# One core, three transformer blocks: the query and key stage of block 1 reordered, and the delta rule's row terms of block 2 made inside its projections

## The reference, cut to what matters

```python
# block 1: sparse attention beside a convolution
h = rms_norm(x, norm_mix_g)
(q, kc, vc, ks_, vs_, kw, vw, g_nsa, u_a, u_b, g_attn, g_conv) = split(h @ w_in)
q = apply_partial_rope(q)                  # 16 heads of 64; the keys kc, ks_, kw (4 heads of 64) too
k_c = silu((blocks_of_32(rope(kc)) + cmp_k_pos) @ cmp_k_w1) @ cmp_k_w2     # 31 compressed keys
v_c = silu((blocks_of_32(vc) + cmp_v_pos) @ cmp_v_w1) @ cmp_v_w2
attn = nsa_attention(q, k_c, v_c, rk(ks_), rv(vs_), rk(kw), rv(vw), gates)
conv = conformer_conv(u_a, u_b, ...)       # depthwise, 31 taps over time
# block 2: gated delta rule, 8 heads of 128
qkv = silu(causal_depthwise_conv(qkv, conv_w))       # 4 taps, 3072 channels
q = l2norm(q) * 128 ** -0.5;  k = l2norm(k)
g = -exp(a_log) * softplus(a_raw + dt_bias);  gc = cumsum(g)      # per chunk, token and head
decay = exp(gc[..., :, None] - gc[..., None, :])
m = tril(einsum(k * beta, k) * decay)                # solved per chunk, then a scan over chunks
```

## Time and profile before

| what | value |
|---|---|
| median of 3 runs | 2946.54 us (2945.48 to 2947.42) |
| the profiled execution | 2947.61 us, of which the span of the profile is 2945.8 us |
| PE busy | 2751.6 us, 93% |
| DVE busy | 1635.0 us, 56% |
| ACT busy | 1010.9 us, 34% |
| POOL busy | 1053.5 us, 36% |
| mean granted TensorE clock | 0.976 |

### The profile page before, as it was taken

One profiled execution on the slowest core, in us unless ns is written; L12 is line 12 of the kernel. 1 busy time (PEld: TensorE's weight loads), 2 busy tenths in 40 slices (PEclk: granted clock), 3 DMA queues, 4 the chain that ended last, 5 costly groups with the idle time before them and its releaser, 6 DMA issues.

```text
span 2945.8 us, 38330 instructions
## 1 busy us (share of the span) xinstructions
PE 2751.6 (93%) x13198; PEld 2259.6 (77%) x13198; DVE 1635.0 (56%) x2597; ACT 1010.9 (34%) x1750; POOL 1053.5 (36%) x463
## 2 busy tenths in 40 slices
PE   7998899999999989969998999999899999999997
PEld 5875788777888867858887777787577777778775
DVE  6967887573423376556656645435623446653353
ACT  3224555543222253433334411112425553211133
POOL 3432000144444434333423344444332224444443
PEclk9999999999999999989999999999899999999998
DMA  3242000133222222211102222222131112222222
GB/s 127 100 132 68 22 15 15 36 108 102 93 93 99 93 85 83 86 69 62 62 33 79 95 93 92 93 86 92 66 101 58 49 52 93 93 93 93 93 93 86
DMA packets 66296, 234.31 MB, mean 80 GB/s; under 512 B 7515, under 2 KB 9860, under 8 KB 66188
## 3 DMA queue, kind: packets, MB, share of 16 engines
q1 hardware_dynamic: 58176, 211.84, 20.9%
q10 hardware_dynamic: 8012, 21.05, 2.1%
HBM read 228.61 MB, written 2.16 MB: 78 GB/s over the span
## 4 chain that ended last, share of the span: by engine, by line
issue 52%; PE 33%; POOL 12%; DVE 2%; POOLq 0%; ACT 0%; DMA 0%; DVEq 0%; SPq 0%; ACTq 0%
POOL w_lo L405 11%; PE bank L2281 9%; PE bank L2283 9%; PE bank L2282 9%; PE bank L2773 2%; PE bank L2762 2%; PE bank L2460 0%; PE bank L2690 0%; POOLq L409 0%; PE bank L2443 0%; DVE big L1644 0%; PE bank L2811 0%; PE bank L2812 0%; PE bank L2797 0%; DVE big L1646 0%
## 5 line engine op out<-in xcount | busy, mean ns | idle before, releaser
L405 POOL TENSOR_TENSOR w_lo<-raw,w_hi 128x1024 fp32r<-128x1024 f32 x398 | 980.4, 2464 | 1825.9 <-ACT w_hi L496 1686.2
L2281 PE MATMUL bank<-act,w_hi 128*128 128x512 f32 x3128 | 1262.7, 404 | 94.1 <-POOL w_lo L405 26.6
L2283 PE MATMUL bank<-act,w_lo 128*128 128x512 f32 x3128 | 1232.7, 394 | 0.0
L2282 PE MATMUL bank<-act,w_hi 128*128 128x512 f32 x3128 | 1231.6, 394 | 0.0
L2281 PEld LDWEIGHTS bank<-act,w_hi 128*128 128x128 f32 x3128 | 595.6, 190 | 251.6 <-issue 91.3
L496 ACT CAST w_hi<-raw 128x1024 fp32r<-128x1024 f32 x397 | 416.4, 1049 | 939.9 <-PE bank L2283 937.6
L2283 PEld LDWEIGHTS bank<-act,w_lo 128*128 128x128 f32 x3128 | 595.3, 190 | 128.4
L2282 PEld LDWEIGHTS bank<-act,w_hi 128*128 128x128 f32 x3128 | 597.0, 191 | 118.9 <-issue 2.9
L1486 DVE TENSOR_TENSOR X<-X,bank 128x512 f32 x56 | 38.5, 688 | 250.1 <-PE bank L2283 250.0
L1823 DVE CAST act<-tmp 128x512 f32 x64 | 142.2, 2223 | 10.0 <-DVE tmp L1819 5.2
L1598 DVE SCALAR_TENSOR_TENSOR bank<-big,cols,bank 128x512 f32<-128x512 f32 x174 | 115.4, 753 | 0.0
(11 more groups left out here) (388 smaller groups left out, 2895.3 us busy)
## 6 DMA issues: line engine op xcount, KB each, us to landing
raw<-in_w_dram SPq DMA_DIRECT2D x402, 512.0 KB, 3.2
act_f<-head_rows ACTq DMA_DIRECT2D x8, 768.0 KB, 4.1
act_f<-in_cw1k_dram ACTq DMA_DIRECT2D x4, 512.0 KB, 4.2
out_dram<-X ACTq DMA_DIRECT2D x4, 512.0 KB, 2.7
cst<-in_consts_dram ACTq DMA_DIRECT2D x3, 648.5 KB, 4.2
X<-in_x_dram ACTq DMA_DIRECT2D x2, 512.0 KB, 6.3
X<-in_x_dram SPq DMA_DIRECT2D x2, 512.0 KB, 6.0
X<-big ACTq DMA_DIRECT2D x8, 128.0 KB, 2.3
```

Source lines behind the costliest of these rows:

```text
L405: pool.tensor_tensor(w_lo[:, u], raw[:, u].rearrange("p (k n) -> p k n", k=KT), w_hi[:, u].bitcast(F32), ALU.subtract).then_inc(w_lo_ready, 1)
L2281: pe.matmul(o, l_hi, r_hi, start=start, stop=False)
L2282: pe.matmul(o, l_hi, r_lo, start=False, stop=False)
L2283: return pe.matmul(o, l_lo, r_hi, start=False, stop=stop)
```

## The change

**Block 1.** The weights come in another order (`QK_ORDER`): keys and values to be compressed, then the other keys, then the queries. The swap of a chunk stands on PE behind the unit that follows the chunk's own, its rope on DVE another place later, both inside the `qk` stage; the last swap stands in `token_major`. DVE keeps the swapped chunk's product in the swap's own bank and reads the cosines from bank 7, into which ACT copies them, for the first 12 ropes. The 16 transfers of pairs are issued by ACT behind the copies 4 to 7, four each. Blocks with positions are made in four parts at places 10 to 13. Between the ropes stand 60 taps; the 48 that remain stand behind the low query parts, six each. PE's wait for the taps moves from the first compressed sum to the attention. The sums of the compression are in banks 6 and 7, and two parts of the values' sum stand ahead of the keys' sum. ACT makes the high query parts 7 to 2 inside `token_major` and 1 and 0 before the compression.

**Block 2.** `conv4` sums in banks 6 and 7; chunks 22 and 23 are done alone. `LAG` is 3; squares are summed two units earlier; the logarithms stand behind copy 19, the turning of rows on PE behind unit 21, the copies of the rows on ACT (three, from banks 2, 3, 4) behind silu 18, with the store. The loads of rows for heads 0 and 1 stand behind copy 22. The exponentials `BE`, `EGLAST`, `EGLC` stand behind the last silu. `tokens_and_scores(h)` waits for silu 17 + h.

```diff
-ROPED = [12, 13, 10, 11, 8, 9, 0, 1, 2, 3, 4, 5, 6, 7]
-SWAPS = ((2, 3, 4), (5, 6, 7), (8, 9), (10, 11), (12, 13))
+QK_ORDER = [12, 13, 14, 15, 8, 9, 10, 11, 0, 1, 2, 3, 4, 5, 6, 7]
+ROPED = [n for n in QK_ORDER if n < 14]
...
 # ACT, block 1
+                a.wait_ge(rope_table, 3)
+                a.copy(bank[7][:], COS).then_inc(rope_table, 1)
...
+                for j, chunk in enumerate(QK_ORDER):
+                    U = FIRST["qk"] + j
+                    if j:
+                        split_hi(U + 1, (U + 1) % 2)
+                    a.wait_ge(mm_done, U + 1)
+                    a.activation(QK[:, chunk], bank[U % 2][:], ACT.Copy, scale=DH ** -0.5 if chunk < 8 else 1.0).then_inc(act_read, 1)
+                    if 4 <= j < 8:
+                        a.wait_ge(roped, 2)
+                        for g in (2 * (j % 2), 2 * (j % 2) + 1):
+                            pairs_of_positions((j - 4) // 2, g)
+                    if j >= 8 and j % 2 == 0:
+                        keys_weights((j - 8) // 2)
...
                 token_major("token_major", 5, lambda k: [(V_TOK[:, k], slice(0, P))],
-                            lambda k: ACT.Sigmoid if k == 4 else ACT.Copy, lambda k: pairs_of_positions() if k == 0 else None,
-                            whole=True)
+                            lambda k: ACT.Sigmoid if k == 4 else ACT.Copy,
+                            lambda k: [query_high(n) for n in ((), (), (7, 6), (5, 4), (3, 2))[k]], whole=True)
...
+                query_high(1)
+                query_high(0)
                 a.wait_ge(cmp_sum, 1)
                 hidden_by_position(0)
...
 # ACT, block 2
-                LAG = 5
+                LAG = 3
...
+                    if k == 22:
+                        split_hi(U + 2, U % 2)
+                        a.wait_ge(rows_out, 16)
+                        load_rows(0)
+                        load_rows(1)
                     if k >= LAG:
                         silu(k - LAG)
-                    if k == 22:
+                    if k == 19:
                         tables(LOG_EXP)
                         a.wait_ge(l2_sum, 16)
...
                         tables(SILU)
+                    if k == 21:
+                        a.wait_ge(rows_tr, 1)
+                        for x in range(3):
+                            a.copy(ROWS[0:8, x], bank[2 + x][0:8, :]).then_inc(rows_kept, 1)
+                        a.wait_ge(rows_kept, 3)
+                        a.dma_start(head_rows, ROWS[0:8]).then_inc(rows_out, 16)
...
 # DVE, block 1
-                conv_taps(PER_GATE * (KT - 2), EARLY, in_psum)
...
+                def rope(k):
+
+                    chunk, swapped_k = ROPED[k], bank[2 + k % 2][:]
                     v.wait_ge(swapped, k + 1)
-                    v.tensor_tensor(tmp[:, k % 2], bank[2 + k % 2][:], SIN, ALU.mult).then_inc(rope_sin, 1)
-                    link(v.tensor_tensor(QK[:, chunk], QK[:, chunk], COS, ALU.mult))
+                    v.tensor_tensor(swapped_k, swapped_k, SIN, ALU.mult).then_inc(rope_sin, 1)
+                    link(v.tensor_tensor(QK[:, chunk], QK[:, chunk], bank[7][:] if k < 12 else COS, ALU.mult))
                     v.wait_ge(rope_sin, k + 1)
-                    v.tensor_tensor(QK[:, chunk], QK[:, chunk], tmp[:, k % 2], ALU.add).then_inc(roped, 1)
+                    v.tensor_tensor(QK[:, chunk], QK[:, chunk], swapped_k, ALU.add).then_inc(roped, 1)
+
+                for j in range(16):
...
+                    with_rope = j >= 2 and QK_ORDER[j - 2] < 14
+                    if with_rope:
+                        rope(ROPED.index(QK_ORDER[j - 2]))
+                    if 10 <= j < 14:
+                        blocks_with_positions((j - 10) // 2, j % 2)
+                    n = 7 - 3 * with_rope - 4 * (10 <= j < 14)
+                    conv_taps(taken, taken + n, in_psum)
+                    taken += n
+                rope(12)
+                rope(13)
...
                     ins.then_inc(q_lo_made, 1)
+                    n = -(-(EARLY - taken) // (8 - i))
+                    conv_taps(taken, taken + n, in_psum)
+                    taken += n
...
 # DVE, block 2 (conv4_at does the same taps with acc for tmp[:, b])
+                            conv4_at(k, j, bank[6 + b][:])
...
+                def conv4_alone(k):
+
+                    v.wait_ge(act_read, reads + 5 + k + 1)
+                    for j in range(4):
+                        if j:
+                            v.wait_ge(conv4_tap, 3 * k + j)
+                        conv4_at(k, j, bank[6 + k % 2][:])
+                    v.wait_ge(conv4_done, k + 1)
...
 # PE, block 1
+                for j in range(16):
+                    pe.wait_ge(act_read, base + max(j - 1, 0))
+                    unit(first + j, (first + j) % 2, A)
+                    if j and QK_ORDER[j - 1] < 14:
+                        pe.wait_ge(act_read, base + j)
+                        swap(ROPED.index(QK_ORDER[j - 1]))
+                c.add("act_read", 16)
+                token_major("token_major", 5, lambda k: swap(13) if k == 0 else None)
...
-                pe.wait_ge(conv_done, KT * 3 // 4)
...
+                pe.wait_ge(tok_kept, 5)
+                values_part(0)
+                values_part(1)
+                pe.wait_ge(early_in, 32 + 64)
+                for n in range(16):
+                    ins = one_chunk(0, n, CW1K[:, n])
+                ins.then_inc(cmp_sum, 1)
+                values_part(2)
...
                 pe.wait_ge(q_lo_made, 8)
+                pe.wait_ge(conv_done, KT * 3 // 4)
...
 # PE, block 2
-                    if 6 <= k < 22:
-                        length_squares(k - 6)
+                    if 4 <= k < 20:
+                        length_squares(k - 4)
...
+                    if k == 21:
+                        pe.wait_ge(rows_made, 2)
...
-                        pe.wait_ge(silu_done, 24)
+                    pe.wait_ge(silu_done, 17 + h)
```

More of the change, by code:

```diff
@@ L983, in block_2 @@
                 tables(LOG_EXP)
[L984 to L990, removed]
+                a.wait_ge(rows_made, 2)
+                a.activation(BE, BE, ACT.Exp)
+                a.activation(EGLAST, GL, ACT.Exp)
+                a.activation(EGLC, EGLC, ACT.Exp).then_inc(decays, 1)
                 def row_decay(h):
@@ L1641, in block_1 @@
-                for k, chunk in enumerate(ROPED):
+                    for j in range(8 * half, 8 * half + 8):
+                        ins = v.tensor_scalar(BLOCKS[:, m, j], X[:, 4 * m:4 * m + 4, 2 * j:2 * j + 16 * 30 + 1:16],
+                                              col(1, "cmp_pos", 16 * m + j), None, ALU.add)
+                    ins.then_inc(blocks_made, 1)
+                    v.wait_ge(blocks_made, 2 * m + half + 1)
+                def rope(k):
+                    chunk, swapped_k = ROPED[k], bank[2 + k % 2][:]
@@ L2443, in swap @@
                     pe.matmul(bank[2 + k % 2][:], const(1, "swap", 128), QK[:, ROPED[k]], start=True, stop=True).then_inc(swapped, 1)
-                swap(0)
-                swap(1)
-                token_major("token_major", 5, lambda k: [swap(n) for n in SWAPS[k]])
+                first, base = FIRST["qk"], c["act_read"]
+                banks_free()
+                for j in range(16):
[6 more added lines that the diff above has]
+                token_major("token_major", 5, lambda k: swap(13) if k == 0 else None)
                 def turn_hidden(m):
@@ L2481, in block_1 @@
                     ins.then_inc(mm_done, 1)
+                pe.wait_ge(tok_kept, 5)
[6 more added lines that the diff above has]
+                values_part(2)
+                pe.wait_ge(roped, 14)
+                pe.wait_ge(hidden_ready, 1)
+                turn_hidden(0)
+                values_part(3)
+                pe.wait_ge(hidden_ready, 2)
+                for mt in range(2):
+                    ins = pe.matmul(bank[6][:, 0:124], CW2K[:, mt], HID[:, 0, mt], start=mt == 0, stop=mt == 1)
+                ins.then_inc(cmp_sum, 1)
                 pe.wait_ge(hidden_ready, 3)
```

132 lines of the change are left out of this document (45 added, 87 removed).

## The result

The changed kernel takes 2922.28 us (median of 4, 2919.52 to 2925.07) against 2946.04 (median of 4 beside it): ratio 0.9919, 95% interval 0.9903 to 0.9935. The forecast was 2922.5 us. Its profiled execution took 2921.11 us, 26.5 less than the one of before; the medians differ by 23.8.

A forecast was written before the change was run, and what follows sets the result against it. PE, busy 93%, was taken to bound most stages, leaving only holes of some 4 + 15 + 17 us; 2947.61 - 10.7 - 13.5 = 2923.4 us profiled, less 1.07 for the median, rounded 2922.5; range 2918 to 2926 (57%).

The forecast's parts named there:

- The `qk` stage: Block 1: 13 swaps at 1.0 us each make this stage end 13 us later, at 215.7 us, with DVE keeping pace.
- The 16 transfers: Block 1, `qk` stage: ACT's issuing of them delays PE 0.1 us at each of four places, taken as 0.5 us.
- The rounds: Block 1, before the attention: DVE runs eight low pairs with six taps each, 5.36 us apiece, 42.9 together, to 274 us.
- rival *slower: Block 1: taps between low parts take longer; whole change breaks even at 1.17 us a tap; 2949 us, chance 2%.
- PE's stall: Block 1, before the compression: PE waits from 245.3 to about 251.6 us, behind ACT's wait at `query_high(2)`.
- The attention's start: Block 1: attention begins at 291.4 us against 302.6, a gain of 11.2, minus 0.5, so 10.7 us; bounds 3 and 15.
- with all meetings: Block 1: if DVE's work before the attention meets POOL throughout, it starts at 291 to 293 us; without any, 287.9.
- PE's waits: Block 2, `qkv` stage: PE waits 1.2 us at unit 21 and 0.9 us at unit 23 for rounded weights.
- the loads: Block 2: rows for head 0 are issued at 1273.9 us, 13.6 us sooner; DVE's first solve gains 13.5 us.
- POOL's chain stays last, by 1.4 us: Block 2, before head 0's solve: POOL's additions and `decay` end at 1286.5 us, the last silu's side at 1285.0.
- `conv4` in banks: Block 2: sums in banks 6 and 7 avoid POOL; that DVE work lay under PE's, so costed at nothing.
- The sum: Whole kernel: 2947.61 - 10.7 - 13.5 = 2923.4 us profiled; median 1.07 us lower, 2922.3, rounded 2922.5.

The follow-up runs named there:

- early split: Against the changed kernel, block 2's weights of units 21 and 23 are rounded directly behind copies 19 and 21; 2918.72 us, ratio 0.9912.

## Why the prediction was right

The total was right, and so were most of its steps, with two errors of opposite sign in the parts. That the median met the forecast to 0.2 us is luck: the kernel's own executions spread by 5.5 us, the parts were missed by -0.7 and +1.3 us, and a term put at nothing was worth 2.6. Differences of some tenths in what follows are read from single profiles and are not more certain than the scatter given above.

- **The `qk` stage.** Predicted 100.1 us to its end at 215.7, measured 98.67: a place with a swap takes 6.37 us, so a swap costs 0.93 us, not 1.0. The 16 transfers showed in one of their four places, 157.25 - 150.62 = 6.63 against 6.37, 0.26 us of the 0.5 that I took.
- **The rounds.** Predicted 5.36 us each and gapless, measured 5.49 and 1.6 us more in the first two together, the meetings that I had costed at 1.5 behind the rounds: DVE is through at 276.1 instead of 275.5. They are the chain up to there: twelve taps more moved the attention by 7.2 us. Behind them it is nearly a tie, since DVE still waits 0.7 to 2.2 us for ACT before the last low keys. The rival *slower* needed 1.17 us a tap; the rows show 4.05 / 6 = 0.68.
- **PE's stall** at `query_high(2)`: predicted 6.3 us and off the path; measured 6.63, and taking it away gained nothing.
- **The attention's start.** Predicted gain 10.7, measured 10.0. Two small errors cancel (eight rounds of 0.13 us more, 13 swaps of 0.07 less); what is left is that I took 291.4 from the 291 to 293 us "with all meetings", and as much came: masks 3.03 us, low keys 279.95 to 293.52 with ACT's 0.74 us among them. Over the profiles with this block 1 the gain is 8 to 11 us, so that the 0.7 us have no weight.
- **Block 2, PE's waits.** Predicted 1.2 and 0.9, measured 1.36 and 0.47. By the Trainium skill ("ScalarE: Activation LUTs", What ACT_TABLE_LOAD costs) a load of 1.283 us has a drain of 1.38 us beside it, and by my estimate from these figures the first wait would have been 4.0 us. The load at 1243.90 takes 1.28 us and the logarithm follows at 1245.19, the second load at 1245.53 is followed by the rounding at 1246.82: no drain is seen, and the measurement decides.
- **Block 2, the loads.** Predicted 13.6 us sooner against the stage, measured 15.1 (1287.55 - 1129.37 against 1263.08 - 1119.96). I had put the issue behind the rounding of 1.05 us; the queue issued it with the copy. So POOL came first, and the step "POOL's chain stays last, by 1.4 us" is the one that failed: ACT's side was predicted at 1275.6 on this axis and came at 1275.96, POOL's at 1277.1 and came at 1275.55. The mistake was the loads' issue, and it was in the kernel's favour: the gain was 14.8 us instead of 13.5, and by the rows would have been 0.4 more but for the silus' side. With the early split the silus come sooner still, and POOL is last again (`decay` waits 0.41 us for it).
- **`conv4` in banks**, costed at nothing: wrong at the stage's end, where it is worth 2.6 us. The last chunk's four taps stand ahead of the last silu, with no PE work to cover them; they took 5.5 us in SBUF (from 1273.78 us) and 3.1 in banks (from 1269.88). The earlier trace rows had the price of a tap that meets POOL, and I should have charged it to these four.
- **The sum**: 10.7 + 13.5 = 24.2 predicted, 24.8 measured in the two parts. The other 1.7 us of the profiled executions' difference lie in code that was hardly touched, and are less than its scatter.

## What to carry to other kernels

Where two engines take turns in front of a stage, count what else stands in these turns: 12 extra taps cost 7.2 of the 8.1 us that they take, and taking 36 away paid only until ACT and PE became the chain (8.8 of 22 us). The kernel with fewer taps took 2912.4 us both times, some 10 us less than the changed kernel. Price an edit that only removes meetings between engines where its stage ends, not where it is busy: `conv4` in banks is worth 2.6 us in the last units, the ropes in banks nothing in the middle of a full stage. And follow a gain to the end of the kernel before adding it up: of the 1.5 to 1.9 us that the early split won ahead of the solve nothing could be found at the end.

## What was not expected of the hardware

- A DMA that the program has behind a rounding was issued at 1263.08 us, 0.4 us ahead of that rounding (1263.47), and one behind a table load and three exponentials with the silu ahead of them (1274.95). In both the issue ran ahead of work of its own engine.
- Behind one and the same stall of PE of 3.6 us the clock fell in each of seven profiles, but for a different time: for 8 matmuls with ropes in SBUF and with fewer taps (twice), for 13 or 14 in the three with the early split and in the kernel before. Two profiles of one kernel agree. The length of a stall does not by itself say what it costs; why the spell is longer in some kernels was not tried.
- Where DVE and POOL both worked on SBUF at the same time, both were slower: two `conv4` taps took 3.56 and 3.11 us instead of 1.55, POOL's addition 1.38 instead of 1.05.
